# Experts of a mixture-of-experts layer in blocks of 32 rows on four column tiles, instead of 64 rows on two

## The reference

```python
h = modulate(rmsnorm(x, g_ffn), sh2, sc2)            # (1024, 1024)
grp = argmax(h @ w_group + b_group)                   # one of 4 groups
e_in = (h @ w_router + b_router)[grp's 8 experts]
top_v, top_i = top_k(e_in, 2)                         # 2 of the group's 8 experts
gate_w = softmax(top_v) * p_grp
eid = grp * 8 + top_i                                 # 32 experts in all
...
hid = silu(xb @ w_e_gate[e]) * (xb @ w_e_up[e])       # (rows, 1024) @ (1024, 512)
y = hid @ w_e_down[e]                                 # (rows, 512) @ (512, 1024)
...
x = x + gt2 * (sum over a token's 2 experts of gate_w * y)
out = rmsnorm(x, g_final)
```

## Time and profile before

| | |
|---|---|
| median of 3 runs | 1893.2 us (1892.54 to 1893.57) |
| the profiled execution's own time | 1891.99 us |
| its span, from the first to the last instruction | 1889.7 us |
| PE busy | 1676.3 us, 89% of the span |
| DVE, ACT, POOL busy | 983.7, 494.4, 193.4 us |
| bytes moved | 325.53 MB, mean 172 GB/s |
| granted TensorE clock, mean | 0.956 |

### The profile page before, as it was taken

One profiled execution on the slowest core, in us unless ns is written; L12 is line 12 of the kernel. 1 busy time (PEld: TensorE's weight loads), 2 busy tenths in 40 slices (PEclk: granted clock), 3 DMA queues, 4 the chain that ended last, 5 costly groups with the idle time before them and its releaser, 6 DMA issues.

```text
span 1889.7 us, 22655 instructions
## 1 busy us (share of the span) xinstructions
PE 1676.3 (89%) x7893; PEld 868.0 (46%) x7894; DVE 983.7 (52%) x1928; ACT 494.4 (26%) x976; POOL 193.4 (10%) x370
## 2 busy tenths in 40 slices
PE   1997899999998886999999999399999989999881
PEld 1662365564644553666666455233333333333330
DVE  6467548888887556456655433433333333333225
ACT  2115344554444665010110111011111111111112
POOL 0010000000000000000000000112222212222210
PEclk9898999999998998999999999599999999999995
DMA  8562321010000102111211812689989737999987
GB/s 284 180 222 78 106 73 45 23 46 1 1 1 1 57 1 67 34 34 33 67 33 44 326 67 105 268 331 399 395 319 399 281 122 261 400 399 363 405 336 284
DMA packets 114583, 325.53 MB, mean 172 GB/s; under 512 B 15240, under 2 KB 53128, under 8 KB 89936
## 3 DMA queue, kind: packets, MB, share of 16 engines
q1 hardware_dynamic: 102768, 296.79, 41.2%
q0 software_dynamic: 11744, 27.79, 6.0%
HBM read 293.33 MB, written 31.23 MB: 172 GB/s over the span
## 4 chain that ended last, share of the span: by engine, by line
PE 78%; DVE 8%; DMA 6%; ACT 5%; issue 2%; SPq 1%; DVEq 0%; ACTq 0%; POOLq 0%; POOL 0%
PE ps L1214 18%; PE ps L1154 9%; PE ps L1232 9%; PE ps L1015 6%; PE ps L1143 6%; PE ps L1168 6%; PE ps L1040 3%; DMA arena<-in_w_e_up_dram 3%; PE ps L1021 3%; PE ps L1091 3%; PE ps L969 3%; PE ps L1065 3%; PE ps L1051 2%; DVE arena L1399 2%; PE ps L1208 2%
## 5 line engine op out<-in xcount | busy, mean ns | idle before, releaser
L1214 PE MATMUL ps<-arena 128*64 128x512 f32 x1632 | 379.4, 608 | 18.4 <-DMA arena<-in_w_e_up_dram 10.7
L1741 DVE COPY arena<-ps 128x256 f32<-128x256 f32 x51 | 21.7, 425 | 396.4 <-ACT arena L900 396.4
L1214 PEld LDWEIGHTS ps<-arena 128*64 128x64 f32 x1632 | 115.9, 139 | 235.2 <-issue 228.1
L1232 PE MATMUL ps<-arena 128*64 128x512 f32 x816 | 186.4, 598 | 0.5 <-ACT arena L904 0.5
L1154 PE MATMUL ps<-rounded 128*128 128x512 f32 x768 | 183.3, 398 | 0.0
L1417 DVE TENSOR_SCALAR_CACHE_REDUCE arena<-arena,small 128x384 bf16<-128x384 f32 (+2 forms) x204 | 182.0, 939 | 0.0
L1154 PEld LDWEIGHTS ps<-rounded 128*128 128x128 f32 x768 | 144.2, 188 | 36.6 <-issue 7.7
L1143 PE MATMUL ps<-arena 128*128 128x512 f32 x256 | 115.4, 604 | 12.9 <-DVEq L1587 12.9
L701 POOL DMA_INDIRECT sum_rows<-arena,ones x51 | 81.4, 1595 | 438.7 <-DVE arena L1763 429.9
L1015 PE MATMUL ps<-arena 128*128 128x512 f32 x256 | 117.1, 611 | 4.8 <-ACT arena L764 3.4
L1065 PE MATMUL ps<-arena 128*64 128x128 f32 x1152 | 96.5, 287 | 26.4 <-ACT arena L798 22.8
(11 more groups left out here) (267 smaller groups left out, 1918.8 us busy)
## 6 DMA issues: line engine op xcount, KB each, us to landing
arena<-in_w_e_gate_dram SPq DMA_DIRECT2D x32, 2048.0 KB, 14.6
arena<-in_w_e_up_dram SPq DMA_DIRECT2D x32, 2048.0 KB, 20.2
arena<-in_w_e_down_dram SPq DMA_DIRECT2D x32, 2048.0 KB, 15.5
arena<-in_w_mod_dram SPq DMA_DIRECT2D x12, 2048.0 KB, 8.7
arena<-in_w_in_dram SPq DMA_DIRECT2D x33, 512.0 KB, 4.5
arena<-in_x_dram SPq DMA_DIRECT2D x16, 512.0 KB, 12.3
arena<-sum_rows SPq DMA_DIRECT2D x16, 512.0 KB, 10.5
sum_rows<-arena SPq DMA_DIRECT2D x2, 2304.0 KB, 16.4
```

Of the source, the lines that this page charges most:

```text
L1214: m = pe.matmul(ps[o * TB:(o + 1) * TB, 2, 0:2 * FQ].rearrange("p (j n) -> p j n", j=2), xT[:, k % NX, k // NX * TB:(k // NX + 1) * TB], w ...
L1232: m = pe.matmul(ps[o * TB:(o + 1) * TB, 5, 0:DQ], hidT[:, k % NH_T, k // NH_T * TB:(k // NH_T + 1) * TB], w_dn[c][:, k, o * DQ:(o + 1) * D ...
```

## The change

NT goes from 2 to 4. With it TB becomes 32, DQ 256, FQ 128, NX (transposes of a block's rows) 2, NH_T (of its hidden rows) 1, AHEAD 8, BLOCKS 96, ROWS 104, and RUN, which is S // TB, 32. A block has 128 pieces of 256 columns where it had 128 of 512.

The order of K changes so that a partition reads one piece of 16 KB per gate and up load; down keeps two of 8 KB. h2 is stored with its columns in that order: DVE writes them permuted (L1636), adds an sh2 that was permuted once by a new copy (ahead of L1547, so that mbc_ok counts ten steps), and the router's weights are loaded in the same order. Gate and up read every second column of a half of the weights, so that one transpose of the hidden rows fits the order in which w_down is loaded.

```diff
-NT = 2
+NT = 4
...
+        sh2_p = at(13, U)
...
-            sp.wait_ge(mbc_ok, 9)
+            sp.wait_ge(mbc_ok, 10)
...
-            sp.dma_start(wgr[:, :, 0:NG], w_group[0].rearrange("(t q) n -> q t n", q=P), allow_slow_non_contiguous=True).then_inc(r_in, 16)
+            sp.dma_start(wgr[:, :, 0:NG], w_group[0].rearrange("(q t) n -> q t n", q=P), allow_slow_non_contiguous=True).then_inc(r_in, 16)
...
-                    sp.dma_start(w_gu[c][:, j].rearrange("p (q t) n -> p q t n", q=NT),
-                                 w[0, ORDER[e]:ORDER[e] + 1].rearrange("o (q p t) n -> p (o q) t n", q=NT, p=P)).then_inc(wgu_in[c], 16)
+                    sp.dma_start(w_gu[c][:, j],
+                                 w[0, ORDER[e]].rearrange("(p t) n -> p t n", p=P)).then_inc(wgu_in[c], 16)
...
-                sp.dma_start(w_dn[c].rearrange("p (q t) n -> p q t n", q=NT),
-                             w_e_down[0, ORDER[e]:ORDER[e] + 1].rearrange("o (q p t) n -> p (o q) t n", q=NT, p=P)).then_inc(wdn_in[c], 16)
+                sp.dma_start(w_dn[c].rearrange("p (q t) n -> p q t n", q=2),
+                             w_e_down[0, ORDER[e]].rearrange("(q p t) n -> p q t n", q=2, p=P)).then_inc(wdn_in[c], 16)
...
-            pe.wait_ge(mbc_ok, 9)
+            pe.wait_ge(mbc_ok, 10)
...
-                rows_t = xrow.rearrange("r (p t) -> r t p", t=NX)
+                rows_t = xrow.rearrange("r (t p) -> r t p", t=NX)
...
-                                      xT[:, k % NX, k // NX * TB:(k // NX + 1) * TB], w_gu[c][:, :, k, o * FQ:(o + 1) * FQ],
+                                      xT[:, k % NX, k // NX * TB:(k // NX + 1) * TB], w_gu[c].rearrange("p j k (q n t) -> p j k q t n", q=2, t=2)[:, :, k, o // 2, o % 2, :],
...
-                dve.tensor_tensor(acc[2 + n // 2][:, half], ps[:, 7, :], bmb[:, n // 2, half], ALU.add).then_inc(mbc_ok, 1)
+                dve.tensor_tensor((sh2_p if n // 2 == 1 else acc[2 + n // 2])[:, half], ps[:, 7, :], bmb[:, n // 2, half], ALU.add).then_inc(mbc_ok, 1)
...
+                dve.tensor_copy(sh2.rearrange("q (k p) -> q p k", k=KT), sh2_p.rearrange("q (p k) -> q p k", k=KT)).then_inc(mbc_ok, 1)
                 dve.scalar_tensor_tensor(a2, a2, 1.0, gffn, ALU.add, ALU.mult).then_inc(mbc_ok, 1)
...
-                link(dve.scalar_tensor_tensor(h2[t % 2], x1[:, t, :], rstd[:, t:t + 1], a2, ALU.mult, ALU.mult))
+                link(dve.scalar_tensor_tensor(h2[t % 2].rearrange("q (k p) -> q p k", k=KT), x1[:, t, :].rearrange("q (p k) -> q p k", k=KT),
+                                              rstd[:, t:t + 1], a2.rearrange("q (p k) -> q p k", k=KT), ALU.mult, ALU.mult))
```

More of the change, by code:

```diff
@@ L537, in _ @@
                 sp.dma_start(x1[:, t, :], x_v[t]).then_inc(x_in[t], 16)
-            sp.dma_start(wgr[:, :, 0:NG], w_group[0].rearrange("(t q) n -> q t n", q=P), allow_slow_non_contiguous=True).then_inc(r_in, 16)
-            sp.dma_start(wgr[:, :, NG:NG + NE], w_router[0].rearrange("(t q) n -> q t n", q=P), allow_slow_non_contiguous=True).then_inc(r_in, 16)
+            sp.dma_start(wgr[:, :, 0:NG], w_group[0].rearrange("(q t) n -> q t n", q=P), allow_slow_non_contiguous=True).then_inc(r_in, 16)
+            sp.dma_start(wgr[:, :, NG:NG + NE], w_router[0].rearrange("(q t) n -> q t n", q=P), allow_slow_non_contiguous=True).then_inc(r_in, 16)
             sp.dma_start(bgr[:, 0:NG], b_group[0:1, :].to_broadcast([P, NG])).then_inc(r_in, 16)
```

## The result

The changed kernel takes **2202.95 us** (median of 4 runs, 2199.12 to 2209.2), the kernel before 1892.87 us (4 runs, 1890.28 to 1893.57). The ratio is 1.1644, with a 95% interval of 1.1615 to 1.1674: 310 us slower. The prediction had said slower, but by 92 us (1985), and its range ended at 2062.

The account below looks back on a forecast made before the run. PE was taken as the bound, weight loads close behind. Terms -105.8-1.5+160.1+40.8+23-22.8+4.5 gave +98; the walk with overlaps gave +87+4.5 = +91.5, taken as 1985 us, range 1955 to 2062.

Parts of the forecast that it names:

- today's loop stays on the chip: PE's loop over experts: instruction packets came in its first pass, 1222 to 1300 us, and none from 1300 to 1838.
- A block of 32 rows: Expert stage on PE: 6.22 us per block, 79 blocks against 51 of 11.71 us, -105.8 us.
- the first rival: Expert-stage matmuls: four tiles don't keep pace, a block takes 7.8 us and the time is 2088 us; chance 0.12.
- The burst of eight pairs: Attention stage: eight weight-load and matmul pairs, weight loads within 0.42 us, 53 ns each; taken as 54 ns per pair.
- Empty passes: PE's queue after seven large experts: 182 passes at 0.737 us, plus 8.5 and 17.5 for slow clock, +160.1 us.
- The other changes of expert: PE's queue between experts, 24 changes: Ifs and value loads show 1.7 us each beyond down's cover, +40.8 us.
- The clock after gaps: PE's first matmuls after long gaps run slower: 17.5 us behind seven loops, 7 behind weight waits.
- Weight waits: PE waiting for expert weights: four waits, 16.4 us, and 7 for the clock after them, +23 us.
- Small edits: Larger tables, the sh2 copy, DVE steps and the permuted h2 write outside the expert blocks: +4.5 us together.
- a stage that I had at +87: Expert stage by a walk through the list of experts, letting waits and gaps overlap: +87 us before the small edits.
- The rival that came true: PE's loop over experts: longer code is fetched again, one or two waits per change, +27 to +75, 2012 to 2060; chance 0.17.
- The third rival: PE's queue at L1262: empty passes cost nothing, hidden behind 34 us of weight waits, 1860 us; chance 0.04.

Follow-up runs that it names:

- experiment 1: Changed kernel with PE's register loop running from 3 to the expert's own number of blocks, without inner If or empty passes, still four block copies per expert: 2078.98 us.
- experiments 1 and 4: Besides experiment 1: the kernel of experiment 2 with its loop fixed from 1 to 32 and the inner If kept, so 418 empty passes: 2145.28 us.
- experiment 2: Changed kernel without empty passes and with two copies of a block's code per expert instead of four: 1852.01 us.
- experiment 7: Kernel before, 64-row blocks: with two copies and no empty passes 1882.81 us; with the change's layout alone 1887.15 us; with both 1876.72 us.
- experiment 6: Kernel before with one more block copy in one or two of its loop's three experts: 13 copies 1896.94 us, 14 copies 2058.66 us.

## Why the prediction was wrong

The direction was right and the size was not: +310 us, where I had +92. The step that failed is the one that let "today's loop stays on the chip" (read correctly from the queue of instructions) stand for a loop with 1.8 times the code, and that priced the failure of it, as a rival, at one or two waits of some 2 us per change of expert. By its terms, against what the profile after shows:

- **A block of 32 rows: right.** 6.22 us predicted, 6.25 measured. Four column tiles keep the rate over whole blocks, so the first rival falls. The burst of eight pairs was the right row to go by.
- **Empty passes: right.** 182 x 0.737 + 8.5 = 142.6 us predicted. The gaps after the seven loops have 151.9, though with some fetching in them; taking the passes away gave back 124 (experiment 1), 0.68 to 0.70 us each (experiments 1 and 4). L1264 was evaluated 203 = 7 x 29 times, as foreseen.
- **The other changes of expert: wrong.** 24 x 1.7 = 40.8 us predicted; the profile has 221.2 in 25 places, +180. The If chain isn't the reason. With the code on the chip (experiment 2) 22 gaps sum to 20.3 us, 0.9 each, though with two Ifs fewer, so even 1.7 looks high. And where the changed kernel walks three copies without a jump over code, its changes of expert take 0.8 to 0.9 us too.
- **The clock after gaps: too small.** The stage's 939 us, less 79 x 6.25 = 494 of blocks and 373 of gaps, leave 72 us, where I had 17.5 + 7. The clock is low after 28 of the 32 gaps, not only after seven loops and four waits: some 3.6 in place of 1.99 us for the first half alone, 28 times 1.6, is 45 of it. Another 6 is a gap ahead of the stage's last transpose, which is no matter of the clock. +47.
- **Weight waits:** 16.4 us predicted, none found, since the other gaps let every load catch up. -16.
- **Small edits:** +4.5 predicted. The part of it that isn't for the larger tables, the copy and the permuted write (+1.2, up to 3.8), came out together with the longer pieces of the loads (-1 predicted) 5.4 us faster on blocks of 64 rows (experiment 7). The sign of that part was wrong. The loads took 1.4% less of the DMA engines' time per byte; that this carries all of the 5.4 us isn't shown, and the copy wasn't timed by itself.

+180 + 9 + 47 - 16 = +220 on a stage that I had at +87, against 939 - 627 = +312 measured. That closes the sum to some 5 us.

Taken together, the other terms of the forecast came out near: 1852 us (experiment 2) and the 124 us of the passes (experiment 1) make an estimate of 1976 us for the change if nothing were fetched again, inside the range, where I had 1985.

**The rival that came true** was priced at 2012 to 2060 with a chance of 0.17. Its mechanism was right, with all its signs; its price wasn't. Without the empty passes, the fetches cost 227 us between experiments 1 and 2, net of the 48 us of waits for weights that came back, where I had 27 to 75: about 7 us per change of expert (248.7 - 20.3 us over 31) and the slow clock behind most. My price came from one branch of 2065 ns, which is one fetch, half hidden. Here two taken branches wait 3.2 and 6.1 us in one change, and PE has 1 us of work left when the first begins. I also gave too little weight to code that grows 1.8 times where nothing in the trace showed room for it. The third rival's price, 1860 without the passes' cost, is near what experiment 2 came to (1852). Its condition, passes hidden behind waits for weights, wasn't met, and the nearness is in part luck: the waits were 48 us and not 34, the changes of expert 20 and not 41.

The Trainium skill (Runtime: NRT & Kernel Launch, "Instruction fetch mechanics") says that a taken branch out of the held pages stalls until its target is fetched. The trace agrees: these are the branches of 3.2 and 6.1 us. The two held pages of 16 KB that the prediction took from it aren't what PE shows: seven packets of 16 KB (0.11 MB) came while the loop of 1296 block instructions made its first pass, and none from 1300 to 1838, and 1404 still stayed (experiment 6). The same section of the Trainium skill gives PE 128 KiB, or 2048 instructions, which the prediction passed over. The limit found here, between 1404 and 1512 without the jumps, waits and loads of registers, lies nearer to that figure; that it is the same limit isn't shown.

**What the change is worth by itself:** at 1852 us, the kernel of experiment 2 is 1.3% under the one with the same loop and layout and blocks of 64 rows (1876.7). The rewrite gives 10 us (experiment 7), the layout 6, the blocks of 32 rows 25. Those blocks would save 106 us of array time, but the stage then runs at the weights' pace, with the DMA engines busy for 0.92 of its 582 us.

Left open: what of a pass's 0.7 us goes where; how many of the fetched packets a given jump needs; why 14 copies cost more than 15; and whether the threshold is one of size alone.

## What to carry to other kernels

Count the instructions of a loop's body for each engine before you make the blocks smaller: halving a block nearly doubles the code of each unrolled copy, and if the queue of instructions then brings packets after the first pass, unroll less. A register loop that runs to a fixed maximum with an If inside pays for each empty pass, so loop to the count that was loaded. And when a profile shows that something "stays" at today's size, that is no evidence for twice the size: give the threshold a chance and price it by every jump over code that would wait, with the slow clock behind it.

## What the runs showed of the hardware

- On PE, a loop of 1404 block instructions (13 copies) ran without fetching again, with 9 packets of instructions in the stage; 1512 (14 copies) brought 91 packets and cost 162 us. The kernel before, with 1296, has 9 packets there too. The jumps' and loads' instructions are not in these counts.
- In a change of expert whose code was fetched again, two branches took 3.2 and 6.1 us where 0.2 is usual, and PE was idle for 10.1 us. In the changed kernel such changes left PE idle for 4 to 19 us, and for 0.8 to 0.9 us where three copies were walked straight through.
- An empty pass of `Fori` with an `If` takes 0.74 us on PE's queue and cost 0.68 to 0.70 us of the time, whether or not the code around it was fetched again.
- 32 pairs of a weight load with 32 columns and a matmul of 256 moving columns, in f32 on four column tiles, take 1.93 to 2.02 us at a granted clock of 1.00. From one group's start to the next the 96 pairs of a block take 5.6 of its 6.25 us, 59 ns a pair, block after block.
- Weights in pieces of 16 KB per partition for gate and up instead of two of 8 KB (down as before) took 1.4% less of the DMA engines' time per byte: 71.6% for 159.54 MB against 72.5% for 159.35 MB in 538 us.
